# Block attention of a prompt on one core: weights turned unnormalised, the division made on the output tile

## What is computed

```python
def attend_chunk(args):
    q_c, sel_c, val_c, pos_c = args
    kg = kb[bi, hi, sel_c].astype(jnp.float32)
    vg = vb[bi, hi, sel_c].astype(jnp.float32)
    logits = jnp.einsum('bhqd,bhqnkd->bhqnk', q_c, kg) * scale
    kpos = sel_c[..., None] * MOBA_BLOCK + offs
    mask = val_c[..., None] & (kpos <= pos_c[None, None, :, None, None])
    logits = jnp.where(mask, logits, NEG)
    w = jax.nn.softmax(logits.reshape(bsz, nh, qc, nsel * MOBA_BLOCK), axis=-1).reshape(logits.shape)
    return jnp.einsum('bhqnk,bhqnkd->bhqd', w, vg)
```

## Time and profile before

| | |
|---|---|
| median of 3 runs | 1871.77 us (1870.25 to 1883.65) |
| the profiled execution | 1887.05 us, span 1885.3 us |
| TensorE busy | 1787.7 us, 95% of the span |
| VectorE, ScalarE busy | 60%, 39% |
| chain that ended last | TensorE 86%, VectorE 8%, ScalarE 2% |
| the attention stage of layer 0 | from the fence near 211 us to the fence near 328 us |

### The profile page before, as it was taken

The page is one execution under the profiler, slowest core; times in us unless marked ns, Lnnn a source line. Parts: engine busy times, 40 slices in busy tenths (PEclk is TensorE's granted clock), DMA queues, the critical chain, the costliest instruction groups (busy, mean ns, idle before and its releaser), DMA issues.

```text
span 1885.3 us, 34376 instructions
## 1 busy us (share of the span) xinstructions
PE 1787.7 (95%) x13464; PEld 1622.6 (86%) x13464; DVE 1134.8 (60%) x2371; ACT 734.1 (39%) x1321; POOL 36.0 (2%) x65
## 2 busy tenths in 40 slices
PE   6899798999999999999999998888999999999997
PEld 5789455999999999989799985445999999999997
DVE  7975356568777762256525855666468777762264
ACT  5222335553333342256323323656553333342253
POOL 1400000000000000000000000000000000000000
PEclk9999788999999999999999996989999999999999
DMA  4124577313222232132121142863313222132111
GB/s 182 66 28 163 204 267 288 112 43 100 79 88 78 64 132 81 47 118 79 51 95 57 57 150 96 313 225 122 111 35 98 81 79 88 54 136 79 71 64 51
DMA packets 77953, 204.18 MB, mean 108 GB/s; under 512 B 12530, under 2 KB 14882, under 8 KB 77314
## 3 DMA queue, kind: packets, MB, share of 16 engines
q1 hardware_dynamic: 75762, 190.36, 29.8%
q0 software_dynamic: 2064, 12.06, 1.7%
HBM read 190.81 MB, written 10.40 MB: 107 GB/s over the span
## 4 chain that ended last, share of the span: by engine, by line
PE 86%; DVE 8%; ACT 2%; issue 2%; DMA 2%; SPq 1%; DVEq 0%; ACTq 0%; POOLq 0%
PE psum L412 29%; PE psum L1946 15%; PE psum L606 13%; PE psum L2346 7%; PE psum L2303 3%; PE psum L420 3%; PE psum L1408 2%; PE psum L1383 2%; PE psum L865 2%; PE psum L2496 1%; PE psum L526 1%; PE psum L540 1%; PE psum L1492 1%; PE psum L1520 1%; PE psum L2559 1%
## 5 line engine op out<-in xcount | busy, mean ns | idle before, releaser
L412 PE MATMUL psum<-sb_a_sb_r,sb_ring_r 128*128 128x288 f32 x1408 | 297.6, 296 | 0.0
L412 PE MATMUL psum<-sb_a_sb_r,sb_arena_r 128*128 128x288 f32 x1344 | 276.5, 296 | 0.0
L412 PE MATMUL psum<-sb_y_sb_r,sb_ring_r 128*128 128x288 f32 x960 | 263.3, 299 | 0.6 <-DVE sb_ring_r L372 0.6
L412 PEld LDWEIGHTS psum<-sb_a_sb_r,sb_ring_r 128*128 128x128 f32 x1408 | 231.3, 188 | 0.3
L372 DVE TENSOR_TENSOR sb_ring_r<-sb_ring,sb_ring_r 128x1024 fp32r<-128x1024 f32 (+1 forms) x90 | 116.2, 1295 | 177.7 <-ACT sb_ring_r L369 176.7
L412 PEld LDWEIGHTS psum<-sb_a_sb_r,sb_arena_r 128*128 128x128 f32 x1344 | 217.0, 188 | 0.0
L412 PE MATMUL psum<-sb_y_sb_r,sb_arena_r 128*128 128x288 f32 x704 | 207.2, 294 | 6.3 <-DVE sb_a_sb_r L372 6.2
L369 ACT ACTIVATE sb_ring_r<-sb_ring 128x1024 fp32r<-128x1024 f32 (+1 forms) x90 | 99.9, 1114 | 289.2 <-PE psum L412 172.3
L412 PEld LDWEIGHTS psum<-sb_y_sb_r,sb_ring_r 128*128 128x128 f32 x960 | 175.5, 190 | 1.5 <-DVE sb_ring_r L372 1.0
L369 ACT ACTIVATE sb_arena_r<-sb_ring 128x1024 fp32r<-128x1024 f32 x90 | 92.9, 1055 | 171.6 <-PE psum L412 149.5
L606 PE MATMUL psum<-sb_arena_r 128*128 128x288 f32 x960 | 156.9, 297 | 1.0 <-DVE sb_arena_r L372 0.9
(11 more groups left out here) (406 smaller groups left out, 3176.3 us busy)
## 6 DMA issues: line engine op xcount, KB each, us to landing
sb_ring<-w SPq DMA_DIRECT2D x166, 512.0 KB, 3.5
sb_ring<-wd SPq DMA_DIRECT2D x32, 704.0 KB, 4.2
sb_arena<-sb_v SPq DMA_DIRECT2D x64, 256.0 KB, 5.3
sb_arena<-moba_v SPq DMA_DIRECT2D x56, 256.0 KB, 5.3
sb_ring<-moba_k SPq DMA_DIRECT2D x32, 256.0 KB, 5.6
sb_a_sb<-moba_k SPq DMA_DIRECT2D x32, 256.0 KB, 7.5
sb_ring<-sb_k SPq DMA_DIRECT2D x32, 256.0 KB, 6.0
sb_a_sb<-sb_k SPq DMA_DIRECT2D x32, 256.0 KB, 6.5
```

The costliest lines, as they stand in the source:

```text
L412: ins = e.eng.matmul(out[:, half, :], fr(w[p][:, k, :]), fr(x[q][:, k, cols]), start=(first and k == 0 and i == 0), stop=(last and k == kb ...
```

## The change

- The exponentials are turned as they are, undivided. TensorE turns them back into the PSUM bank in which the scores of the same unit stood. The scores take three banks in rotation, where they took two beside two for the turns. The scores of a unit wait until the turned weights of the unit three before are copied; before, they waited for the exponential of the unit two before.
- TensorE's step now does the turns first and the scores of the next unit behind them.
- In the output the operands are exchanged: the turned weights are stationary (128 columns), the values move (64 columns). It comes out with queries on the partitions, the heads of a pair side by side in one bank, one head after the other.
- VectorE divides by the row sum there: for each of the 16 pairs of units one reciprocal of two columns and two multiplications of 128 x 64 out of PSUM into `onb`, in place of 32 reciprocals and 32 multiplications of up to 128 x 512.
- TensorE turns the divided tile (one turn for each pair), ScalarE copies it into `y`: 16 copies of 128 x 128 in place of four of 128 x 512.
- The loop has five steps more at its end, for the last pair of units.

```diff
@@ -1472,13 +1472,18 @@
-        stat = small[:, 8:64]
-
-        sco_ready, nmx_ready, prob_ready, pn_ready, ptr_ready, pt_ready, o_unit, o_copied = (
-            sem(x) for x in ("sco_ready", "nmx_ready", "prob_ready", "pn_ready", "ptr_ready", "pt_ready", "o_unit", "o_copied"))
-        UNITS = [(2 * c + hh, i) for c in range(4) for i in range(4) for hh in range(2)]
+        onb = [cut(unit_at + 6 * 512 + i * P, P) for i in range(2)]
+        assert unit_at + 6 * 512 + 2 * P <= 27952
+        most, nmost, total, share = (small[:, 8 + 8 * i:16 + 8 * i] for i in range(4))
+
+        sco_ready, nmx_ready, prob_ready, ptr_ready, pt_ready, o_unit, o_normed, o_turned, o_copied = (
+            sem(x) for x in ("sco_ready", "nmx_ready", "prob_ready", "ptr_ready", "pt_ready", "o_unit", "o_normed",
+                             "o_turned", "o_copied"))
+        PAIRS = [(c, i) for c in range(4) for i in range(4)]
+        UNITS = [(2 * c + hh, i) for c, i in PAIRS for hh in range(2)]
 
         DUE_A = {"pe": (8, (1, 2, 6, 7, 8, 9)), "act": (8, (5, 5, 6)), "dve": (8, (3, 4, 5, 9, 9))}
+        LAST_A = len(UNITS) + 5
 
 ...
             def scores(u):
                 hh, i = UNITS[u]
                 r0, c, n = 64 * (hh % 2), hh // 2, P * (i + 1)
-                if u >= 2:
-                    pe.wait_ge(prob_ready, u - 1)
-                pe.matmul(psum[:, u % 2, 0:n], zqk[r0:r0 + 64, c, i * P:(i + 1) * P], zqk[r0:r0 + 64, 4 + c, 0:n],
+                if u >= 3:
+                    pe.wait_ge(pt_ready, u - 2)
+                pe.matmul(psum[:, u % 3, 0:n], zqk[r0:r0 + 64, c, i * P:(i + 1) * P], zqk[r0:r0 + 64, 4 + c, 0:n],
                           start=True, stop=True).then_inc(sco_ready, 1)
 
-            def outputs(u):
-                c, i = UNITS[u][0] // 2, UNITS[u][1]
-                pe.wait_ge(pt_ready, u + 2)
-                if i == 0 and c >= 1:
-                    pe.wait_ge(o_copied, c)
-                for j in range(i + 1):
-                    for x in (u, u + 1):
-                        hh = UNITS[x][0]
-                        r0 = 64 * (hh % 2)
-                        last = pe.matmul(psum[r0:r0 + 64, 4, i * P:(i + 1) * P],
-                                         vt[:, j, hh * HD:(hh + 1) * HD], ptb[x % 4][:, j, :],
-                                         start=(j == 0), stop=(j == i))
-                        if j == i:
-                            last.then_inc(o_unit, 1)
+            def turned(u):
+                pe.wait_ge(prob_ready, u + 1)
+                for j in range(UNITS[u][1] + 1):
+                    last = pe.transpose(psum[:, u % 3, j * P:(j + 1) * P], pb[u % 2][:, j * P:(j + 1) * P], ident)
+                last.then_inc(ptr_ready, 1)
+
+            def outputs(p):
+                c, i = PAIRS[p]
+                pe.wait_ge(pt_ready, 2 * p + 2)
+                if p >= 2:
+                    pe.wait_ge(o_copied, p - 1)
+                for hh in range(2):
+                    at = (2 * c + hh) * HD
+                    for j in range(i + 1):
+                        last = pe.matmul(psum[:, 3 + p % 2, HD * hh:HD * hh + HD], ptb[(2 * p + hh) % 4][:, j, :],
+                                         vt[:, j, at:at + HD], start=(j == 0), stop=(j == i))
+                    last.then_inc(o_unit, 1)
+
+            def output_turned(p):
+                pe.wait_ge(o_normed, p + 1)
+                pe.transpose(psum[:, 3 + p % 2, P:2 * P], onb[p % 2], ident).then_inc(o_turned, 1)
 
             scores(0)
-            for u in range(len(UNITS) + 2):
-                if u + 1 < len(UNITS):
-                    scores(u + 1)
+            scores(1)
+            for u in range(LAST_A + 1):
                 if 1 <= u <= len(UNITS):
-                    hh, i = UNITS[u - 1]
-                    pe.wait_ge(pn_ready, u)
-                    if u >= 3:
-                        pe.wait_ge(pt_ready, u - 2)
-                    for j in range(i + 1):
-                        last = pe.transpose(psum[:, 2 + (u - 1) % 2, j * P:(j + 1) * P],
-                                            pb[(u - 1) % 2][:, j * P:(j + 1) * P], ident)
-                    last.then_inc(ptr_ready, 1)
-                if u >= 3 and u % 2 == 1:
-                    outputs(u - 3)
-                between(samples, u, len(UNITS) + 1, DUE_A["pe"])
+                    turned(u - 1)
+                    if u + 1 < len(UNITS):
+                        scores(u + 1)
+                if u % 2 == 1:
+                    p = u // 2
+                    if 1 <= p <= len(PAIRS):
+                        outputs(p - 1)
+                    if 2 <= p <= len(PAIRS) + 1:
+                        output_turned(p - 2)
+                between(samples, u, LAST_A, DUE_A["pe"])
         def act_moba_prompt(e):
             act = e.eng
 
-            def copy_out(c):
-                act.wait_ge(o_unit, 8 * (c + 1))
-                act.activation(y[:, 4 + c, 0:TP], psum[:, 4, :], ACT.Copy).then_inc(o_copied, 1)
+            def copy_out(p):
+                c, i = PAIRS[p]
+                act.wait_ge(o_turned, p + 1)
+                act.activation(y[:, 4 + c, i * P:(i + 1) * P], psum[:, 3 + p % 2, P:2 * P], ACT.Copy).then_inc(o_copied, 1)
 
             act.wait_ge(stored, 16 * 5)
-            for u in range(len(UNITS) + 1):
+            for u in range(LAST_A + 1):
                 if u < len(UNITS):
-                    hh, i = UNITS[u]
-                    n = P * (i + 1)
+                    n = P * (UNITS[u][1] + 1)
                     act.wait_ge(nmx_ready, u + 1)
                     if u >= 2:
                         act.wait_ge(ptr_ready, u - 1)
-                    act.activation(pb[u % 2][:, 0:n], psum[:, u % 2, 0:n], ACT.Exp, scale=ATT_SCALE,
-                                   bias=stat[:, 2 + u % 2:3 + u % 2], accum_out=stat[:, 4 + u % 2:5 + u % 2])\
+                    if u >= 8:
+                        act.wait_ge(o_normed, (u - 8) // 2 + 1)
+                    act.activation(pb[u % 2][:, 0:n], psum[:, u % 3, 0:n], ACT.Exp, scale=ATT_SCALE,
+                                   bias=nmost[:, u % 4:u % 4 + 1], accum_out=total[:, u % 8:u % 8 + 1])\
                        .then_inc(prob_ready, 1)
                 if u == len(UNITS):
 ...
-                if u >= 1:
-                    hh, i = UNITS[u - 1]
+                if 1 <= u <= len(UNITS):
+                    i = UNITS[u - 1][1]
                     act.wait_ge(ptr_ready, u)
                     if u >= 5:
                         act.wait_ge(o_unit, u - 4)
-                    act.activation(ptb[(u - 1) % 4][:, 0:i + 1, :], psum[:, 2 + (u - 1) % 2, 0:P * (i + 1)]
+                    act.activation(ptb[(u - 1) % 4][:, 0:i + 1, :], psum[:, (u - 1) % 3, 0:P * (i + 1)]
                                    .rearrange("p (j n) -> p j n", j=i + 1), ACT.Copy).then_inc(pt_ready, 1)
-                if u >= 10 and (u - 10) % 8 == 0:
-                    copy_out((u - 10) // 8)
+                if u >= 6 and u % 2 == 0:
+                    copy_out((u - 6) // 2)
                 if u == len(UNITS):
                     act_slab(e, out_pairs[1], 1)
-                    copy_out(3)
-                between(samples, u, len(UNITS), DUE_A["act"])
+                between(samples, u, LAST_A, DUE_A["act"])
 ...
-            for u in range(len(UNITS) + 1):
+            for u in range(LAST_A + 1):
                 if u < len(UNITS):
-                    hh, i = UNITS[u]
+                    i = UNITS[u][1]
                     n = P * (i + 1)
                     v.wait_ge(sco_ready, u + 1)
-                    own = psum[:, u % 2, i * P:n]
+                    own = psum[:, u % 3, i * P:n]
                     do(v.tensor_tensor(own, own, causal, ALU.add))
-                    do(v.tensor_reduce(stat[:, u % 2:u % 2 + 1], psum[:, u % 2, 0:n], AXX, ALU.max))
-                    if u >= 2:
-                        v.wait_ge(prob_ready, u - 1)
-                    v.tensor_scalar(stat[:, 2 + u % 2:3 + u % 2], stat[:, u % 2:u % 2 + 1], -ATT_SCALE, None, ALU.mult)\
+                    do(v.tensor_reduce(most[:, u % 4:u % 4 + 1], psum[:, u % 3, 0:n], AXX, ALU.max))
+                    if u >= 4:
+                        v.wait_ge(prob_ready, u - 3)
+                    v.tensor_scalar(nmost[:, u % 4:u % 4 + 1], most[:, u % 4:u % 4 + 1], -ATT_SCALE, None, ALU.mult)\
                      .then_inc(nmx_ready, 1)
-                if u >= 1:
-                    w = u - 1
-                    n = P * (UNITS[w][1] + 1)
-                    v.wait_ge(prob_ready, w + 1)
-                    do(v.reciprocal(stat[:, 6 + w % 2:7 + w % 2], stat[:, 4 + w % 2:5 + w % 2]))
-                    v.tensor_scalar(pb[w % 2][:, 0:n], pb[w % 2][:, 0:n], stat[:, 6 + w % 2:7 + w % 2], None, ALU.mult)\
-                     .then_inc(pn_ready, 1)
-                between(samples, u, len(UNITS), DUE_A["dve"])
+                if u >= 4 and u % 2 == 0 and (u - 4) // 2 < len(PAIRS):
```

(11 more changed lines are left out.)

## The result

| | before | changed |
|---|---|---|
| first comparison, median (13 runs each) | 1873.72 us | 1885.24 us (1880.23 to 1890.15) |
| ratio, 95% interval | | 1.0049, 1.0033 to 1.0065 |
| repeated, median (31 and 8 runs) | 1874.87 us | 1881.66 us (1874.80 to 1886.87) |
| ratio, 95% interval | | 1.0035, 1.0017 to 1.0054 |
| profiled execution, span | 1887.05, 1885.3 us | 1880.62, 1878.8 us |

By the ratios the change costs 7 to 9 us, 0.35 to 0.5%; the medians stand 11.5 us apart in the first comparison and 6.8 in the second. That is within 1%, but clearly more than nothing, and by the ratios 1.7 to 2.4 times the 3.9 us of the forecast.

A forecast was written before the change was run, and what follows sets the result against it. Bound: in the attention stage, TensorE late behind VectorE's division (vector stretch), then TensorE without a gap (tensor stretch). 5.0 + 1.5 - 4.0 + 1.4 = +3.9 us, median 1871.77 to 1875.7 us; range 1865 to 1888.

The forecast's parts named there:

- term 1: Long outputs in the tensor stretch: exchanged operands cost +1.25 us a period, +5.0 in all; bounds nothing and +15.2.
- Term 2: Output-tile turns on TensorE in the tensor stretch: eight at 0.19 us, +1.5 us; bounds 0.9 and 2.9.
- Term 3: Vector stretch, end of L1390 to first L1397: -1.0 us a period, -4.0 in all; bounds -8.0 and +2.0.
- rival A: Attention stage: TensorE's idle stretches shrink and the clock stays up; sum -0.1 us, 1871.7 us; chance 0.2.
- Terms 4 and 5: The scores' new wait for ScalarE's copy, and ScalarE's sixteen smaller output copies: both hidden, costing nothing.
- Term 6: End of the attention stage: last division, turn and copy behind the copies L1468; +1.4 us, between 0.8 and 2.4.
- The prediction's own sign: Attention period: 0.6 us longer than before would show the forecast right.
- Rival B: Vector stretch: nothing won, L1397 no sooner than 10.9 us after L1390 ends; sum +7.9, 1879.7 us; chance 0.14.
- Rival C: Tensor stretch: clock stays at 0.50 until the turn, up to 10 us a period, +40 us, 1916; chance 0.06.

The follow-up runs named there:

- e2: Changed kernel with the output's old operands (values stationary, turned weights moving), division and turn kept, output values wrong; 1882.49 us, ratio 1.0029.
- e12: Changed kernel with idle matmuls at the attention's waits, ahead of the last output-tile turn and in the recurrence; 1886.67 us, ratio 1.0058.
- e6: Kernel before with idle matmuls ahead of TensorE's three waits for the division in each attention period; 1873.94 us, ratio 0.9986.
- e9: Kernel before with 44 idle matmuls (24 and 20) ahead of two TensorE waits in the second layer's recurrence; 1884.43 us, ratio 1.0052.
- e10: Changed kernel with 44 idle matmuls in the recurrence; 1896.03 us, ratio 1.0111 against the kernel before.
- e4: Changed kernel without the last division and turn, the last tile copied from PSUM as it is; 1887.08 us, ratio 1.0050.
- e7: Changed kernel with idle matmuls at TensorE's attention waits and ahead of the last output-tile turn; 1878.35 us, ratio 1.0023.
- e5: Changed kernel run and profiled once more, no edit; 1881.66 us, ratio 1.0035 against the kernel before.
- e11: Kernel before with idle matmuls both at the attention's waits for the division and in the recurrence; 1878.73 us, ratio 1.0005.

## Where the forecast held, and which of its steps did not

The measured change lies within 1% and inside the stated range, and by the ratios it is 1.7 to 2.4 times the forecast. The range held by a slip in its top. Two thirds of the way to half clock make term 1 +11.8 (5.0 + 2/3 x 10.2), and the sum then +10.7: 1882.5 us. The forecast instead adds 12 to 1875.7, which has the 5.0 in it already, and comes to 1888. By its own working the 1885.24 us would have been outside; this part is luck.

- **Term 1, exchanged operands, +5.0.** Right. The records grew by 1.48 + 1.93 - 1.83 = 1.58 us a period; the period itself, by e2 at full clock, by 1.3: +5.2. The sum left out two things that nearly cancel: a short group has a fixed part (below), and a turn behind the exchanged form is cheaper.
- **Term 2, turns, +1.5.** A turn takes 0.11 to 0.12 us in e12's tensor stretch: 8 x 0.11 = 0.9, the low bound. I had taken 0.19 from the pair L1416, which stood directly behind outputs of the old form (0.37 us for two). Behind an output tile's turn the same pair takes 0.22.
- **Term 3, the vector stretch, -1.0 a period.** It shrank by 1.3 us. What division and order are worth depends on the clock. At 1.00 it is 10.0 - 9.6 = 0.4 us, as e6 against the changed kernel shows. At 0.78 it is 10.94 - 9.63 = 1.3 us, as e9 against e10's second period shows. The step that failed is that the half clock was taken as given: with the clock at 1.00 in the changed kernel, L1397 and what follows are quicker too (1.09 us against 1.71), and the prediction had this only in its low bound and in rival A. So the profiled stage came out at -0.4 us where the sum had +3.9. The division itself was sized right (0.9 for the old one, 9.6 - 9.1 = 0.5 for the new one; 0.98 and 0.6 forecast).
- **Terms 4 and 5, nothing.** Right: the tensor stretch has no gap.
- **Term 6, the end, +1.4.** Measured +1.3. But what it "lets the fence go" into was not priced: the pause puts the clock at 0.50 and the next stage pays 2.4 us (34.43 against 31.99; 32.0 in e4 and 32.1 in e7, where the pause is gone or filled). In e2, which keeps the pause, it is 1.4 us (33.41). A further 1.5 us lies near 408 us, in the next L606 x96 (14.59 us in the changed kernel, 13.06 before). e5, e10, e7 and e12 have it, e2 and e4 don't, and e6, the kernel before with filling, has it (14.58) though e11 hasn't. So it can't be tied to the pause or to the change.
- **Rival A, the clock stays up.** The profiled stage is this rival: clock 1.00 in three periods, periods 0.6 to 1.1 us *shorter* although they hold more work, and a stage 0.4 us shorter where A said -0.1. The prediction's own sign, a period 0.6 us longer, did not show in the profiles; with the clock at 1.00 in both kernels it is 1.1 us longer (25.7 to 26.8). As a forecast of the time A failed: 3.9 us lie behind the stage, and in variants of the kernel (e2, e4, e10) the clock falls after all.
- **Rival B, nothing won in the vector stretch.** Refuted: 9.6 us, not 10.9.
- **Rival C, the clock goes down in the tensor stretch.** I gave it 0.06 and up to 10 us a period. It happens, in some periods of some executions: e10 and e4 show it, at 2.6 to 4.3 us a period in the worse ones and 1.2 in e10's second, where L1408 keeps its 2.24 us. The argument against it, that the two rounds of L1408 are ordinary matmuls and run at full clock, does not hold: they took 3.48 and 3.92 instead of 2.24 us.

The profiles of the two kernels sum to -0.4 + 3.9 = +3.5 us, close to my +3.9, but by other terms: that agreement is luck. The medians lost 7 to 9. Of the missing 3 to 6 us e10 shows one part, a stage of 122.9 us in an execution like its others (its four times are 1893.6 to 1899.7). How often the plain changed kernel has such a stage can't be told from two profiles, whose executions are both below its median. e12 against e11 puts the work alone, without any of this, at +5.3 us in the stage. What stays open: how the missing part divides between such stages and longer recurrences, since the filling that made the recurrence equal also moved other things.

The Trainium skill, TensorE: Matmul & The Clock Gate, Part 4, says that a turn does not count as busy time for the clock as a matmul does. In the window from 258 us of the changed kernel TensorE does little but turns and scores and is idle for over half, and the clock stays at 1.00:

```profile
258.00:261.00 3.00, 1.44 (x8) 0.69 (x7) 2.61 (x9) 3.00 (x13) 0.00 (x0) 1.00 1.06 384
```

On that alone one would expect a fall here, as before the change; these runs show it only in some periods of some executions.
